# A hybrid mLSTM/GLA decoder block: the last MLP pass in seven products, the GLA state block-diagonal, and some work moved between engines

## The chip, the cores and the metric

The kernel runs on one core of a Trainium2 chip. The metric is the device time of one execution in microseconds (us). A core has five engines that run side by side and wait for each other by semaphores: TensorE (PE in the profile; its weight loads are listed as PEld) multiplies matrices into PSUM, VectorE (DVE) and ScalarE (ACT) work elementwise on PSUM and SBUF, GpSimd (POOL) works on SBUF alone and issues DMAs, SyncE (SP) issues DMAs. Three executions of the kernel before took 2819.16, 2821.59 and 2823.09 us.

## The reference

One decoder block over 2048 tokens of width 1024, all in float32:

1. Token mixing. RMSNorm of x, one combined projection, then two parallel head groups over chunks of tokens: an mLSTM (4 heads of 128, exponential input gate, running-max stabiliser) and a gated linear attention, GLA (4 heads, keys of 64, values of 128). In GLA each head has a state S of 64 x 128. Per chunk the output is o = A v + (q exp(b)) S, where A holds the causal products within the chunk and b the summed log decays, and then S = exp(b_last) S + k_w^T v. Both groups are normed per head and gated; their concatenation goes through w_out and is added to x.
2. Cross-attention on 256 memory rows, added to x.
3. MLP: x = x + square(relu(rmsnorm(x) w1)) w2, hidden width 4096.
4. A final RMSNorm with its own gain.

## The kernel before

The 2048 tokens are worked in four groups of 512 (GROUP); the first three run in a loop, the fourth is emitted with final=True. xres holds the residual rows of a group, four tiles i of 128 rows. Every weight comes as "slabs" of 128 x 512. SP loads them in pairs (512 KB) into raw; ACT copies a slab into w_hi (rounded; split_hi, L905), DVE subtracts that from raw into w_lo (split_lo, L1417 and L1419), and PE takes three matmuls for each product: hi x hi, hi x lo, lo x hi. Both rings have four slabs (RING), and the splits run three slabs ahead (LEAD). Each engine goes through the same numbered slabs, and all other work is written by hand between them: "if s == 49" in an engine's function means that this work is queued on that engine behind its split in slab step s. An engine's queue is strictly in order.

A full slab (slab, L1981) is 12 matmuls of 128 x 128 by 128 x 512: four output tiles by three. The projections of the mixing are slabs 0 to 55; w_out starts with slab 56.

GLA, in slab steps 41 to 53 (G_SLAB = 41, three steps a chunk, four chunks c of 128 tokens a group, so 16 chunks in all). PE's queue in step slot 0 holds, for the chunk before: outputs_start (carried for heads 0 and 2, L2135), state_step (L2166), outputs (carried for heads 1 and 3, L2135, and then the four A v products, L2157), and then levels for the next chunk (L2097, L2100), whose end signals lvl_full. The state stS has the key rows of two heads on the partitions 0 to 63 and 64 to 127, so each product of carried takes 64 rows of the array and 128 columns. DVE's queue in the same step: split_lo, then a wait on o_full and a copy of the output from PSUM into tok (L1744), a wait on s_full and two state updates (L1749), then two level_sum (L1564 multiply and L1568 reduce), which wait on lvl_full. ACT waits for that copy (o_out) and takes four sums of squares (L1226).

The gated mLSTM heads are moved in this way: in step 49, behind its split, DVE gates all four heads (gate_heads, 16 instructions, L1606), each head signalling mixed. POOL waits for all four and then issues 16 DMAs that move blocks of the heads between partitions (move_heads, L687). In step 53 DVE waits until all 16 have landed (heads_in) and transposes 32 x 32 blocks, ACT makes x_hi (L1099), DVE x_lo (L1585); heads 0 and 1 in step 53, heads 2 and 3 in step 54, with the split of step 54 between them. PE waits for the x_lo of all four before it starts slab 56.

The MLP goes over the hidden width in four passes hb of 1024 (LAST is 3). A pass has 16 full slabs for w1, and then h w2. In all passes but the last of the last group, h w2 is done in seven products of quarters (the Strassen-Winograd scheme; P1, P7, P6, P2, P5, P4, P3 in this order). A product is four slabs (product, L2348), each with 6 matmuls (two tiles by three). It needs sums of quarters of the weights (sums_dram, made once by POOL) and of the hidden rows: POOL makes these (hidden_sums) and the lower halves of the operands (operand_low, L727), ACT the upper halves (operand_high, L1306). DVE adds each finished quarter to xres (add_product, L1840) and signals prod_free. The pass is 16 + 28 slabs. The last pass of the last group (mlp_pass) is an ordinary one: 16 slabs for w1 and 16 full slabs for w2 (L1981, and last_chunks, L2329, which finishes one tile of rows after the other).

Behind it comes the final norm of the last group. For each tile i of rows DVE adds the last half (L1935), multiplies by the final gain (L1938), ACT takes the sum of squares of the half (L1092), DVE the variance (L1942), ACT a logarithm and an exponential (L1381, L1383), DVE three small refining steps (L1921 to L1924) and the scaling of one half (L1927), ACT the scaling of the other (L1373), and SP stores the row tile (L592). The first halves were squared and weighed while PE was still at work.

## Time and profile before

| what | value |
|---|---|
| median of 3 executions | 2821.59 us |
| the profiled execution, its device time | 2816.63 us |
| its span, first to last instruction | 2815.1 us |
| PE busy | 2796.2 us (99%) |
| PEld busy | 2328.2 us (83%) |
| DVE busy | 1812.2 us (64%) |
| ACT busy | 1514.2 us (54%) |
| POOL busy | 1054.5 us (37%) |
| mean granted TensorE clock | 0.999 |
| traffic of HBM | 346.24 MB read, 33.59 MB written |

The span is the time from the first to the last instruction of the profiled execution, and the device time lies 1.5 us above it. Busy means that an instruction of the engine is under way; matmuls overlap each other, so the distance between the starts of two matmuls, and not their length, is what one costs. An engine's idle time matters only where PE, or the end, waits for it.

### The profile page before, as it was taken

Reading aid. Unit: us, or ns where it says so; the run is one execution under the profiler, and the core shown is the slowest. Engines: PE = TensorE matmul, PEld = TensorE weight load, DVE = VectorE, ACT = ScalarE, POOL = GpSimd, SP = SyncE. Lnnn points to the kernel's source line nnn. Section 1 sums busy time; section 2 is a strip of 40 time slices with the busy share of each in tenths; the row PEclk is TensorE's granted clock in tenths of the full one; section 3 lists DMA queues with packets and bytes.
Section 4 is the critical chain, followed back from the end, with each engine's and each line's share of the span. In section 5 each row is a group of like instructions: output and inputs, shape, how many; then the busy total and the mean of one; then the engine's idle time right before and its main releaser. Section 6 shows DMA issues by size and latency. Waiting matters only on the chain.

```text
span 2815.1 us, 44964 instructions
## 1 busy us (share of the span) xinstructions
PE 2796.2 (99%) x15076; PEld 2328.2 (83%) x15076; DVE 1812.2 (64%) x3011; ACT 1514.2 (54%) x3126; POOL 1054.5 (37%) x1334
## 2 busy tenths in 40 slices
PE   8999999999999999999999999999999999999998
PEld 8888888888878888888888888888888888888887
DVE  6376764776686755556788675466668675545665
ACT  6555444566655444555565544456655544455553
POOL 5264554665354400234546320044435550013330
PEclk9999999999999999999999999999999999999999
DMA  6732476565552222355554222255455222234442
GB/s 216 251 105 67 173 268 242 186 211 151 149 188 83 76 89 90 108 171 161 164 177 135 69 84 90 90 158 179 143 150 199 81 74 90 90 104 144 151 149 83
DMA packets 185906, 393.41 MB, mean 140 GB/s; under 512 B 14224, under 2 KB 14368, under 8 KB 185664
## 3 DMA queue, kind: packets, MB, share of 16 engines
q1 hardware_dynamic: 160112, 309.89, 35.2%
q0 software_dynamic: 22880, 75.72, 8.0%
q10 hardware_dynamic: 2672, 4.76, 0.5%
q8 instruction: 129, 2.11, 0.3%
q14 instruction: 113, 0.93, 0.1%
HBM read 346.24 MB, written 33.59 MB: 135 GB/s over the span
## 4 chain that ended last, share of the span: by engine, by line
PE 98%; DMA 1%; ACT 0%; DVE 0%; issue 0%; POOL 0%; ACTq 0%; DVEq 0%
PE bank L1981 44%; PE work L1981 22%; PE bank L2348 17%; PE work L2348 3%; PE work L1995 1%; PE bank L2386 1%; PE work L2097 1%; DMA vo_dram<-folded 1%; PE bank L1995 1%; PE work L2135 1%; PE work L2157 1%; PE work L2043 1%; PE work L2246 1%; PE work L2250 1%; PE work L2245 1%; PE work L2229 1%
## 5 line engine op out<-in xcount | busy, mean ns | idle before, releaser
L905 ACT ACTIVATE w_hi<-raw 128x512 fp32r<-128x512 f32 x1156 | 724.7, 630 | 1012.6 <-PE bank L1981 514.5
L1419 DVE TENSOR_TENSOR w_lo<-raw,w_hi 128x512 fp32r<-128x512 f32 x657 | 481.2, 736 | 785.8 <-ACT w_hi L905 784.2
L1417 DVE SCALAR_TENSOR_TENSOR w_lo<-raw,w_hi 128x512 fp32r<-128x512 f32 x499 | 448.8, 921 | 92.6 <-ACT w_hi L905 91.6
L737 POOL TENSOR_TENSOR hr<-qk 128x256 f32<-128x256 f32 x60 | 44.9, 750 | 773.3 <-ACT qk L1293 773.3
L2348 PE MATMUL bank<-w_hi,h_hi 128*128 128x512 f32 x720 | 280.3, 389 | 0.1
L2348 PE MATMUL bank<-w_hi,h_lo 128*128 128x512 f32 x720 | 280.1, 389 | 0.0
L2348 PE MATMUL bank<-w_lo,h_hi 128*128 128x512 f32 x720 | 280.1, 389 | 0.0
L1981 PE MATMUL bank<-w_hi,x_hi 128*128 128x512 f32 x640 | 255.2, 399 | 0.0
L1981 PE MATMUL bank<-w_lo,x_hi 128*128 128x512 f32 x640 | 249.6, 390 | 0.0
L1981 PE MATMUL bank<-w_hi,x_lo 128*128 128x512 f32 x640 | 249.5, 390 | 0.0
L727 POOL TENSOR_TENSOR h_lo<-qk,h_hi 128x256 fp32r<-128x256 f32 x180 | 180.7, 1023 | 71.1 <-ACT h_hi L1306 71.1
L1981 PE MATMUL work<-act_hi,w_hi 128*128 128x512 f32 x512 | 199.2, 389 | 0.0
L1981 PE MATMUL work<-act_lo,w_hi 128*128 128x512 f32 x512 | 199.2, 389 | 0.0
L1981 PE MATMUL work<-act_hi,w_lo 128*128 128x512 f32 x512 | 199.2, 389 | 0.0
L1981 PE MATMUL bank<-act_hi,w_hi 128*128 128x512 f32 x464 | 180.8, 390 | 0.0
L1981 PE MATMUL bank<-act_hi,w_lo 128*128 128x512 f32 x464 | 180.5, 389 | 0.0
L1981 PE MATMUL bank<-act_lo,w_hi 128*128 128x512 f32 x464 | 180.5, 389 | 0.0
L2348 PEld LDWEIGHTS bank<-w_hi,h_hi 128*128 128x128 f32 x720 | 135.1, 188 | 28.8 <-issue 0.7
L2348 PEld LDWEIGHTS bank<-w_hi,h_lo 128*128 128x128 f32 x720 | 135.1, 188 | 28.2
L2348 PEld LDWEIGHTS bank<-w_lo,h_hi 128*128 128x128 f32 x720 | 135.1, 188 | 27.9
L791 POOL TENSOR_TENSOR zz<-zz,gqkv 128x128 f32<-128x128 f32 x224 | 118.0, 564 | 106.8 <-ACT gqkv L1251 106.8
L1981 PE MATMUL bank<-x_hi,w_hi 128*128 128x512 f32 x384 | 152.9, 398 | 0.0
(405 smaller groups left out, 6465.0 us busy)
## 6 DMA issues: line engine op xcount, KB each, us to landing
raw<-in_w_dram SPq DMA_DIRECT2D x226, 512.0 KB, 3.9
raw<-sums_dram SPq DMA_DIRECT2D x120, 512.0 KB, 3.9
raw<-in_w_in_dram SPq DMA_DIRECT2D x112, 512.0 KB, 3.5
raw<-in_w_out_dram SPq DMA_DIRECT2D x32, 512.0 KB, 4.1
raw<-kq_dram SPq DMA_DIRECT2D x32, 512.0 KB, 3.8
raw<-vo_dram SPq DMA_DIRECT2D x32, 512.0 KB, 3.8
xres<-in_x_dram POOLq DMA_DIRECT2D x16, 512.0 KB, 5.9
early_rows<-in_w_dram POOLq DMA_DIRECT2D x8, 1024.0 KB, 8.8
```

The lines of the kernel that those rows point to most:

```text
L727: nc.gpsimd.tensor_tensor(operand(q, h_lo)[:, kt, :], src, operand(q, h_hi)[:, kt, :].bitcast(F32), ALU.subtract).then_inc(operand_lo_pool, 1)
L737: nc.gpsimd.tensor_tensor(diff[:, kt, :], quarter(0, 0, kt), quarter(0, 1, kt), ALU.subtract).then_inc(diff_ready, 1)
L791: ins = nc.gpsimd.tensor_tensor(v[:, :, :, r, :], v[:, :, :, r, :], src, ALU.mult)
L905: nc.scalar.activation(w_hi[:, slot, :], raw[:, pair_slot, slot % 2, :], ACT.Copy).then_inc(slab_hi, 1)
L1417: ins = stt(out=w_lo[:, slot, :], in0=src, scalar=1.0, in1=hi, op0=ALU.mult, op1=ALU.subtract)
L1419: ins = tt(w_lo[:, slot, :], src, hi, ALU.subtract)
L1981: ins = mm(dst, left, right, start=(kt == 0 and j == 0), stop=(kt == KT - 1 and j == 2))
L1995: ins = transpose(into[kt % 4][:, i * P:(i + 1) * P], src[:, i, kt * P:(kt + 1) * P], ident[:])
L2043: ins = mm(wbank[2 + j % 2][:, hh * MEM:(hh + 1) * MEM], left, right, start=(k == 0 and i == 0), stop=(k == 1 and i == 2))
L2097: ins = mm(dst, z, z, start=True, stop=True)
L2135: ins = mm(work[:, 2, cut[hd]], qe[p0:p0 + 64, c % 2, j, :], stS[p0:p0 + 64, j, :], start=(hd == 0), stop=False, skip_group_check=True)
L2348: ins = mm(dst[:], left[:, kt, here], right[:, kt, :], start=(CHAIN_BEFORE[q] is None and kt == 0 and j == 0), stop=(kt == HALF - 1 and j ...
```

## The change

1. The last pass of the last group is a pass of seven products like the others; mlp_pass, last_chunks and their semaphores and tables go. In its last product P3 the order over tiles and slabs is written out, so that tile 0 is complete six matmuls before tile 1. P4 gives the left half of row tiles 2 and 3 and P3 the right half of row tiles 0 and 1; so the rows are finished in the order 2, 3, 0, 1 (LAST_ROWS).
2. POOL multiplies the four halves that are complete early (P2 and P5) by the final gain, behind the hidden sums of the pass. ACT takes their sums of squares in the slab steps 34 and 38. DVE does the halves of P4 in one instruction each (row by scale by gain) and those of P3 as before in two. The final rows lie in x_blocks and no longer in qk.
3. The GLA state stS becomes 128 x 256 for each pair of heads, with zeros off the diagonal. carried is two matmuls of all 128 rows and 256 columns in outputs_start, and nothing of it in outputs. The state update on DVE is four instructions of 64 partitions in place of two of 128.
4. The copy of the GLA output into tok is ACT's, in front of its sums of squares; DVE no longer waits on o_full there.
5. gate_heads for the heads 2 and 3 of the mLSTM is queued in step 50, behind the level sums of that step.

The rest of the diff puts nine small tiles into one, keeps the addresses behind them where they were (SPARE) and drops what is not used any more.

```diff
-FINAL_USES, _ = use_table([KT] * 4)
+LAST_ROWS = (2, 3, 0, 1)
 assert len(USES) == GROUP_SLABS and GROUP_SLABS % (2 * PAIRS) == 0
...
         stC = sb("stC", [P, HEADS, HD + 1])
-        stS = sb("stS", [P, 2, HD])
+        stS = sb("stS", [P, 2, 2 * HD])
...
         x_blocks = sb("x_blocks", [P, NCH, D], F32, mlp)
+        last_rows = x_blocks
         x_turned = sb("x_turned", [P, KT, GROUP], F32, mlp)
...
-                    if hb < LAST or not final:
-                        for name, row, col in WEIGHTS:
-                            if name == "sums":
-                                for k in range(HALF):
-                                    sums_done(sp, HALF * hb + k)
-                            w = sums_dram if name == "sums" else A["w2"]
-                            for kp in range(HALF // 2):
-                                load(g, p, pair_of(w, hb * D + row * COLS + kp * 2 * P, col * COLS))
-                                p += 1
-                    else:
-                        for b in range(2):
-                            for kp in range(KT // 2):
-                                load(g, p, pair_of(A["w2"], hb * D + kp * 2 * P, b * COLS))
-                                p += 1
+                    for name, row, col in WEIGHTS:
+                        if name == "sums":
+                            for k in range(HALF):
+                                sums_done(sp, HALF * hb + k)
+                        w = sums_dram if name == "sums" else A["w2"]
+                        for kp in range(HALF // 2):
+                            load(g, p, pair_of(w, hb * D + row * COLS + kp * 2 * P, col * COLS))
+                            p += 1
...
                 if final:
-                    for i in range(NCH):
-                        sp.wait_ge(tok_ready, PRO_ROWS + 8 * g + i + 1)
-                        sp.wait_ge(half_out, i + 1)
-                        sp.dma_start(out[g * GROUP + i * P:g * GROUP + (i + 1) * P, :], out_rows[:, i, :])\
+                    for k, i in enumerate(LAST_ROWS):
+                        sp.wait_ge(tok_ready, PRO_ROWS + 8 * g + k + 1)
+                        sp.wait_ge(half_out, k + 1)
+                        sp.dma_start(out[g * GROUP + i * P:g * GROUP + (i + 1) * P, :], last_rows[:, i, :])\
                             .then_inc(stored_last, 16)
...
                     hidden_sums(2)
+                    hidden_sums(3)
+                    pool.wait_ge(fin_g_in, 16 * NG)
+                    for q in (Q_P2, Q_P5):
+                        for tile in range(2):
+                            i, here = 2 * ROW_HALF[q] + tile, slice(COL_HALF[q] * COLS, (COL_HALF[q] + 1) * COLS)
+                            pool.wait_ge(prod_free, free_no(g, LAST, q, tile))
+                            nc.gpsimd.tensor_tensor(last_rows[:, i, here], xres[:, i, here], fin_g[:, here],
+                                                    ALU.mult).then_inc(first_half, 1)
                     return
...
-                def sum_half(i, half):
+                def sum_half(i, half, into):
 
                     here = slice(half * COLS, (half + 1) * COLS)
                     nc.scalar.activation(tok[:, i, here], xres[:, i, here], ACT.Square,
-                                         accum_out=(ss, ss_b)[half][:, i:i + 1]).then_inc(half_ss, 1)
+                                         accum_out=into[:, i:i + 1]).then_inc(half_ss, 1)
...
                     if slot == 0 and 1 <= c <= NCH:
 
-                        act.wait_ge(o_out, 4 * g + c)
+                        act.wait_ge(o_full, 4 * g + c)
+                        nc.scalar.activation(tok[:, c - 1, COLS:], work[:, 2, :], ACT.Copy).then_inc(o_out, 1)
...
-                        split(g, MLP_AT[hb] + s)
+                        if not (final and hb == LAST and s + LEAD >= PASS_SLABS):
+                            split(g, MLP_AT[hb] + s)
...
+                        if final and hb == LAST and s in (2 * KT + 18, 2 * KT + 22):
+                            q = Q_P2 if s == 2 * KT + 18 else Q_P5
+                            for tile in range(2):
+                                act.wait_ge(prod_free, free_no(g, LAST, q, tile))
+                                sum_half(2 * ROW_HALF[q] + tile, COL_HALF[q], ss)
                         if final:
...
                     if slot == 0 and 1 <= c <= NCH:
-                        dve.wait_ge(o_full, 4 * g + c)
-                        nc.vector.tensor_copy(tok[:, c - 1, COLS:], work[:, 2, :]).then_inc(o_out, 1)
                         dve.wait_ge(s_full, 4 * g + c)
                         if c >= 2:
                             dve.wait_ge(s_ready, 4 * g + c - 1)
-                        for j in range(2):
-                            ins = stt(out=stS[:, j, :], in0=stS[:, j, :], scalar=eb[:, (c - 1) % 2, j, CH - 1:CH],
-                                      in1=work[:, 3, j * HD:(j + 1) * HD], op0=ALU.mult, op1=ALU.add)
+                        for hd in range(HEADS):
+                            j, k, half = hd // 2, hd % 2, slice(64 * (hd % 2), 64 * (hd % 2) + 64)
+                            own = stS[half, j, k * HD:(k + 1) * HD]
+                            ins = stt(out=own, in0=own, scalar=eb[half, (c - 1) % 2, j, CH - 1:CH],
+                                      in1=work[half, 3, j * HD:(j + 1) * HD], op0=ALU.mult, op1=ALU.add)
                         ins.then_inc(s_ready, 1)
...
                     if s == 49:
                         read_out(dve, g, 4 * B_MO + 3)
                         dve.wait_ge(num_out, 4 * g + 4)
-                        gate_heads(0, HEADS)
+                        gate_heads(0, HEADS, (0, 1))
+                    if s == 50:
+                        gate_heads(0, HEADS, (2, 3))
...
+                    if final and hb == LAST:
+                        return
...
+                def weigh_half(q, tile):
+
+                    i, half = 2 * ROW_HALF[q] + tile, COL_HALF[q]
+                    here = slice(half * COLS, (half + 1) * COLS)
+                    dve.wait_ge(prod_free, free_no(g, LAST, q, tile))
+                    return tt(last_rows[:, i, here], xres[:, i, here], fin_g[:, here], ALU.mult)
+
+                for hb in range(HB):
                     split_pass(hb)
-                if final:
-                    mlp_pass()
-                def last_row(i):
-
+
+                def last_var_of(k):
+
+                    here = slice(LAST_ROWS[k], LAST_ROWS[k] + 1)
+                    dve.wait_ge(half_ss, NCH + k + 1)
+                    stt(out=var[:, here], in0=ss_b[:, here], scalar=1.0 / D, in1=ss[:, here], op0=ALU.mult,
+                        op1=ALU.add).then_inc(last_var, 1)
+
...
+                def last_row(k):
+
+                    i = LAST_ROWS[k]
                     here = slice(i, i + 1)
-                    dve.wait_ge(last_guess, i + 1)
+                    half = slice(COLS, D) if i < 2 else slice(0, COLS)
+                    dve.wait_ge(last_guess, k + 1)
...
+                    dve.wait_ge(last_scale, k + 1)
+                    if k < 2:
+                        dve.wait_ge(prod_free, free_no(g, LAST, Q_P4, k))
+                        stt(out=last_rows[:, i, half], in0=xres[:, i, half], scalar=rstd[:, here], in1=fin_g[:, half],
+                            op0=ALU.mult, op1=ALU.mult).then_inc(tok_ready, 1)
+                    else:
+                        ts(last_rows[:, i, half], last_rows[:, i, half], rstd[:, here], None, ALU.mult)\
+                            .then_inc(tok_ready, 1)
...
+                    dve.wait_ge(fin_g_in, 16 * NG)
+                    dve.wait_ge(half_ss, NCH)
+                    link(ts(ss[:], ss[:], 1.0 / D, EPS, ALU.mult, ALU.add))
+                    last_var_of(0)
+                    last_var_of(1)
+                    for k in range(2):
+                        last_row(k)
+                    add_product(LAST, Q_P3, 0)
+                    add_product(LAST, Q_P3, 1)
+                    link(weigh_half(Q_P3, 0))
+                    last_var_of(2)
+                    link(weigh_half(Q_P3, 1))
+                    last_row(2)
+                    last_var_of(3)
+                    last_row(3)
                     return
...
-                def carried(c, hds):
-
-                    for hd in hds:
-                        j, p0 = hd // 2, 64 * (hd % 2)
-                        ins = mm(work[:, 2, cut[hd]], qe[p0:p0 + 64, c % 2, j, :], stS[p0:p0 + 64, j, :],
-                                 start=(hd == 0), stop=False, skip_group_check=True)
-                    return ins
+                def carried(c, j):
+
+                    return mm(work[:, 2, j * 2 * HD:(j + 1) * 2 * HD], qe[:, c % 2, j, :], stS[:, j, :],
+                              start=(j == 0), stop=False, skip_group_check=True)
...
                     stand_alone(pe)
-                    carried(c, (0, 2)).then_inc(o_even, 1)
+                    for j in range(2):
+                        carried(c, j)
 
                 def outputs(c):
 
                     pe.wait_ge(at_full, 4 * g + c + 1)
-                    pe.wait_ge(o_even, 4 * g + c + 1)
                     stand_alone(pe)
-                    carried(c, (1, 3))
...
+                    if final and hb == LAST and q == Q_P3:
+                        for tile, kt in ((0, 0), (1, 0), (0, 1), (1, 1), (0, 2), (0, 3), (1, 2), (1, 3)):
+                            if kt == 0:
+                                pe.wait_ge(prod_free, free_no(g, hb, Q_P5, tile))
+                            if tile == 0:
+                                pe.wait_ge(slab_lo, slab_no(g, MLP_AT[hb] + 2 * KT + HALF * q + kt + 1))
+                                pe.wait_ge(operand_lo_pool, per_pass(g, N_POOL_LOW, hb, HALF * POOL_LOW[q] + kt + 1))
+                            here = slice(tile * P, (tile + 1) * P)
+                            for j, (left, right) in enumerate(((hi, w_hi), (hi, w_lo), (lo, w_hi))):
+                                ins = mm(chain_bank(q, tile)[:], left[:, kt, here], right[:, kt, :], start=False,
+                                         stop=(kt == HALF - 1 and j == 2), skip_group_check=True)
+                            if kt == HALF - 1:
+                                ins.then_inc(prod_full, 1)
+                        return
```

## Rows read from the trace of the kernel before

**Rows 1.** The page, section 4: the chain that ended last, by engine
```profile
PE 98%; DMA 1%; ACT 0%; DVE 0%; issue 0%; POOL 0%; ACTq 0%; DVEq 0%
```

**Rows 2.** Timeline of PE, a chunk's output: start us, length us, engine, line, instruction, count
```profile
265.07 0.39 PE L1981 MATMUL bank<-w_hi,x_lo 128*128 128x512 f32 x1
265.39 0.71 PE L2135 MATMUL work<-stS,qe 64*128 64x128 f32 x4
266.03 0.66 PE L2166 MATMUL work<-gqkv,kwT 128*64 128x128 f32 x8
266.62 0.71 PE L2135 MATMUL work<-stS,qe 64*128 64x128 f32 x4
267.26 1.16 PE L2157 MATMUL work<-gqkv,sg 128*128 128x128 f32 x8
```

**Rows 3.** Timeline of PE, a slab followed by mLSTM matmuls of the whole array
```profile
193.74 0.39 PE L1981 MATMUL bank<-x_hi,w_lo 128*128 128x512 f32 x1
193.97 1.05 PE L2229 MATMUL work<-qk 128*128 128x128 f32 x8
194.86 0.60 PE L2233 MATMUL work<-ident,qk 128*128 128x128 f32 x4
```

**Rows 4.** Timeline of DVE, slab steps 49 and 50 of the first group
```profile
293.57 4.28 DVE L1606 SCALAR_TENSOR_TENSOR qk<-tok,hscale,qk 128x128 f32<-128x128 f32 x16
...
298.97 0.59 DVE L1749 SCALAR_TENSOR_TENSOR stS<-stS,eb,work 128x128 f32<-128x128 f32 x2
299.49 0.61 DVE L1564 TENSOR_TENSOR mw<-work,lvl_mask 128x448 f32<-128x448 f32 x1
...
301.00 0.62 DVE L1564 TENSOR_TENSOR mw<-work,lvl_mask 128x448 f32<-128x448 f32 x1
```

**Rows 5.** Timeline of PE, the end of the levels in slab step 50
```profile
298.12 0.30 PE L2100 MATMUL work<-gqkv 64*64 64x64 f32 x8
```

**Rows 6.** Timeline of POOL, the moves of the heads; in brackets idle before and releaser
```profile
298.55 10.37 POOL L687 DMA_DIRECT2D qk<-qk  x16 [5.45 <-DVE qk L1606]
```

**Rows 7.** Line L687 by itself, first group: from issue to landing
```profile
DMA to landing us min/median/max: 2.2/2.8/4.4
```

**Rows 8.** Timeline of DVE, slab steps 53 and 54
```profile
313.35 1.30 DVE L1581 STREAM_TRANSPOSE tok<-qk 128x512 f32<-128x512 f32 x2
...
318.35 1.42 DVE L1585 SCALAR_TENSOR_TENSOR x_lo<-tok,norm_g,x_hi 128x512 fp32r<-128x512 f32 x2 [0.20 <-ACT x_hi L1099]
```

**Rows 9.** Timeline of PE, the first matmul of slab 56
```profile
320.22 0.39 PE L1981 MATMUL work<-w_hi,x_hi 128*128 128x512 f32 x1
```

**Rows 10.** Windows behind PE's end: stretch, length, busy by engine, PEclk, DMA share, GB/s
```profile
2807.50:2809.90 2.40, 0.13 (x1) 0.00 (x0) 1.98 (x8) 1.90 (x7) 0.00 (x0) 1.00 0.40 164
2810.10:2815.00 4.90, 0.00 (x0) 0.00 (x0) 1.31 (x5) 1.40 (x2) 0.00 (x0) 0.50 0.68 280
```

**Rows 11.** Timeline of PE, the first matmuls of the kernel
```profile
6.99 3.65 PE L2014 MATMUL work<-ident 128*128 128x128 f32 x16 [6.99 <-ACT tok L948]
```

**Rows 12.** Timeline of PE, the last pass: its first and its last matmul
```profile
2720.43 0.39 PE L2386 MATMUL bank<-act_hi,w_hi 128*128 128x512 f32 x1
...
2807.24 0.39 PE L2329 MATMUL work<-w_hi,h_lo 128*128 128x512 f32 x1
```

**Rows 13.** Timeline of DVE and ACT, last row tile: last refining step, last scaling
```profile
2810.84 0.16 DVE L1924 SCALAR_TENSOR_TENSOR rstd<-y 128x1 f32<-128x1 f32 x1
...
2811.03 0.72 ACT L1373 ACTIVATE qk<-qk,rstd 128x512 f32<-128x512 f32 x1 [0.26 <-DVE rstd L1924]
```

**Rows 14.** Timeline of DVE, the products of the pass before
```profile
2708.67 3.56 DVE L1417 SCALAR_TENSOR_TENSOR w_lo<-raw,w_hi 128x512 fp32r<-128x512 f32 x3
...
2716.47 0.74 DVE L1840 SCALAR_TENSOR_TENSOR xres<-bank,rs_mlp,xres 128x512 f32<-128x512 f32 x1
```

**Rows 15.** Timeline of POOL, its last work in the pass before
```profile
2710.49 4.18 POOL L727 TENSOR_TENSOR h_lo<-hr,h_hi 128x256 fp32r<-128x256 f32 x4
```

**Rows 16.** Lines of POOL by form: busy us, mean ns, then idle before
```profile
L718 POOL TENSOR_TENSOR tok<-tok 128x512 f32<-128x512 f32 x6 | 8.1, 1345 | 0.5
```

153 lines of the change are left out of this document (20 added, 133 removed).

## The prediction

> **What bounds the kernel now.** I read four views in this order. The chain of waits first: 98% of the span is TensorE's own work [rows 1]. So PE's stream of matmuls is the time, plus the tail behind its last matmul; work on the other engines counts only where PE or the tail waits for it. Then PE's timeline around every place that the change touches, then the timelines of DVE, ACT and POOL there, to see how late each handover to PE is, and last the windows behind PE's end. The profiled execution took 2816.63 us (span 2815.1), and the sum is made against it; the median of the runs shown, 2821.59, lies 4.96 above, and I add that at the end.
>
> **The seven products, on PE.** The old last pass has 32 full slabs of 12 matmuls, 384; from its first to its last matmul there are 383 distances in 2807.24 - 2720.43 = 86.81 us, 0.2267 each [rows 12]. The new one has 16 x 12 + 7 x 24 = 360. 24 x 0.2267 = -5.44 us. The chain [rows 1] shows no stall inside the passes of that kind, so I take no stall in the stream itself; the tail is below.
>
> **GLA on PE.** From the last slab matmul before a chunk's output to the A v products it is 267.26 - 265.07 = 2.19 us: 0.96 to L2166, 0.59 for L2166, 0.64 for the second L2135 [rows 2]. The four matmuls of each L2135 (two passes for each of two heads) take 0.64. Eight float32 matmuls of the whole array take 194.86 - 193.97 = 0.89, so 0.111 each, and start 0.23 after the slab [rows 3]. Four at 0.111 would be 0.44: going into and out of the 64-row form costs 0.2 a time. The new carried has four passes of twice the columns, 4 x 0.222 = 0.89, starts 0.23 behind the slab and pays once, 0.09, before L2166: 0.23 + 0.89 + 0.09 + 0.59 = 1.80. Gain 0.39 a chunk, 1.56 a group, 6.2 in all. Bounds: 0 if the passes of 256 columns were slowed as the small forms are, 0.45 if the wider pass saves its fixed part as well. I take 0.39, the rows being of the same form. But this gain only counts if PE does not wait before slab 56, and that is the next part.
>
> **The gating a slab later.** This is the step that decides. PE starts slab 56 at 320.22 [rows 9], and needs the x_lo of all four moved heads. DVE ends the last of them at 318.35 + 1.42 = 319.77 [rows 8]: 0.45 us to spare. The chain before it: gating ends at 293.57 + 4.28 = 297.85 [rows 4]; POOL starts issuing 0.70 later and needs 10.37 for 16 DMAs, one after the other [rows 6]; so the last issue starts at 308.27, and landing takes 2.2 to 4.4 [rows 7], up to 312.7; DVE goes on with the transposes at 313.35 [rows 8], about 0.7 us later.
>
> In the new kernel, in the clock of the old trace:
> - Two chunks are behind PE at step 50, so it is 0.78 early, and the first half of the gating starts near 292.8. A gating instruction is 4.28/16 = 0.27, half are 2.14: 294.9.
> - The split of step 50 takes 0.56 (split and copy share the 1.12 from 297.85 to 298.97 [rows 4]): 295.5. The copy is gone.
> - Four state updates, 0.26 each like the old two (0.52 together): 296.6. Bounds 0.13 (half the partitions, half the time) and 0.30 each.
> - The level sums wait for PE's levels, which end at 298.12 + 0.30 [rows 5], now three chunks of 0.39 earlier: 297.25. Two sums at 301.00 - 299.49 = 1.51 [rows 4]: 300.3.
> - Only now the second half of the gating: 302.4, against 297.85.
> - POOL: + 0.70 + 9.72 to the last issue, 312.8. Landing 2.8 (2.2 to 4.4): 315.6 (315.0 to 317.2).
> - The transposes start 2.3 late; the rest of the chain keeps its 6.42 (313.35 to 319.77), since ACT and DVE have nothing else in it: 322.0. PE starts slab 56 at 322.1.
>
> PE arrives there at 320.22 - 4 x 0.39 = 318.7, so it stands for 3.4 us. Against the old start that is +1.9 a group (0.7 if the level sums do not wait and the landing takes 2.2; 3.5 if it takes 4.4). With four groups: **+7.6 us** (3 to 14), and the 6.2 of GLA are in it already: they are lost in the wait. Behind slab 56 everything is moved by the same amount. ACT now copies the output itself, 0.7 us a chunk, in front of squares for which it had waited for DVE: nothing. The wait of DVE for its level masks in step 51 would also be shorter; that is lost in the same stall.
>
> The clock: behind PE's end the granted clock is still 1.00 for 2.4 us and then 0.50, which is 1.2 GHz in place of 2.4 [rows 10]. A stand of 3.4 us is longer than that. At the start of the kernel 16 transposes took 3.65 us [rows 11], 0.23 each and so twice the 0.111 of rows 3; that stretch at the lower level lost some 1.8 us. I take a fall in three stands of four: 3 x 1.8 = **+5.4** (0 to 7.4). The Trainium skill (TensorE: Matmul & The Clock Gate, section Why this matters for your kernels) says that an idle gap in the middle of a kernel drops the clock to half; by it all four stands would pay, by the old trace taken alone, which has no such gap inside, none need to.
>
> **The last pass's side work and the tail.** Before: from PE's end (2807.24 + 0.23 = 2807.47) the last scaling starts 3.56 later, ends at 4.28, and the execution's span closes at 7.6, so the last store costs 3.3 [rows 12, 13]. In the new kernel, E is the end of PE's stream, and in the pass before E is 2720.43:
> - POOL ends its operands at 2710.49 + 4.18 = E - 5.8 [rows 15] and then weighs four halves. 1.35 each for 128x512 [rows 16], up to 1.8 beside DVE: until about E + 1.
> - While POOL works DVE's splits take 3.56/3 = 1.19 in place of 0.6 [rows 14]; ACT's four extra sums (0.7 each) hold its splits of slabs 38 and 42 by 1.1 to 1.4. Slab 43's lower half comes at about E - 1.7, against a need at E - 2.0; a stall of 0.4 at most, which I leave in the tail.
> - The add of P4 tile 0 starts at 2716.47 = E - 4.0 in the old order [rows 14]; now about E - 1.7, and tile 1 ends at E - 0.35.
> - Then DVE alone, in its written order: variances of rows 2 and 3 (each behind a sum of 0.8 and behind the other's logarithm and exponential on ACT, 0.2 each) until E + 1.3; last_row twice (three small steps of 0.2, one product of 0.7): E + 4.0; two adds of 0.7: E + 5.4; weigh, variance, weigh: E + 7.0; last_row: E + 8.1. Row 3's variance needs ACT's sum, which waits behind the scaling of row 1 in ACT's queue: E + 8.2; logarithm, exponential, three small steps: the last scaling starts at E + 9.4.
> That is 5.9 later than the 3.56 of before. If POOL slows nobody and P4's adds stay at E - 4.0, the same count gives 3.5; if it costs more at each step, 7. I take **+5.3**, near the upper side, because both the queue order and the shared time of POOL and DVE are in rows.
>
> The Trainium skill (GPSIMD Engine Reference, section 1. Specifications) says that POOL shares its SBUF interfaces with DVE when DVE has two SBUF inputs; the 1.19 against 0.6 of the split agrees. By it the weighing on POOL is paid by DVE.
>
> **Sum.** +7.6 + 5.4 - 5.4 + 5.3 = +12.9: 2829.5 for the profiled execution, 2834.5 for the median.
>
> **Rivals.**
> - *The clock holds.* Same stands, no fall. For: no clock below 1.00 inside the old trace. Against: rows 10. Sum +7.5: 2829.1.
> - *The heads still come in time* (the other side). Then PE keeps the 6.2 of GLA and a further 0.2 a group in step 51. This needs the second gating to be over by 298 to 299, so level sums that do not sit in front of it, or DMAs that land 2 us sooner. Against it: DVE's queue is in order, and even with no wait for levels the work in front adds 4.7 us to a chain with 1.2 to spare. Sum -7.0 - 5.4 + 5.3 = -7.1: 2814.5. It decides from a landing before 313.4.
> - *The last pass starves.* POOL's weighing and ACT's sums hold the splits so long that PE waits for slabs 38 to 43 as well, 1 to 1.5 us each for three of them. Against: a slab of a product lasts 6 x 0.2267 = 1.36, and the splits run three slabs, 4.1 us, ahead, so a delay of 1.1 to 1.4 is mostly covered. Sum +12.9 + 4: 2838.5.
> - *The block-diagonal state brings nothing*, because 256 columns cost more than 0.222. It would not show: up to 0.39 a chunk vanishes in the stand before slab 56. It is no case of its own.
>
> **How the numbers follow.** Chances: forecast 0.50, the clock holds 0.25, the heads in time 0.17, starving 0.08. A run of this kernel can tell 0.2%, 5.6 us, from no change. Slower by more: 0.46 of the forecast, 0.17 of the clock case (its lower part, with stands of 2 us, is below 5.6), 0.07 of the starving one: 0.70. Same: 0.04, 0.07, 0.03 and 0.01: 0.15. Faster: 0.14 of the case in time and 0.01: 0.15. The range starts at 2817, which leaves out the better half of the heads case, and ends at 2842 (stands of 4.5 us with four falls and a tail of 7 would be 2846).
>
> **What would show it.** Line L687's 16 issues start some 4.5 us later against PE's slabs, and DVE's transposes wait for a DMA. PE's waits have a new row at the first matmul of slab 56, released by DVE x_lo, four times, 3 to 4 us each; windows there show PEclk below 1.00. L2135 goes, two matmuls with 256 columns stand in its place, 0.9 us in all, and L2166 starts 1.2 after the slab. The last pass has 360 matmuls, and the last scaling starts 9 us after PE's end. The prediction is wrong if PE enters slab 56 without a wait, if a wait is under 2 us, or if the tail is no longer than before.

## The result, and the profile after

The changed kernel takes 2836.19 us (median of 6 runs, 2830.17 to 2839.95), the kernel before 2821.16 (6 runs): ratio 1.0053, 95% interval 1.004 to 1.0066. It is 15.0 us slower; forecast were 12.9. The profiled execution (2839.95 us, span 2838.4) is the longest of the six, 23.3 us above the profiled one of before. That is 8.3 us more than the medians differ by: it lies 3.8 above its own median, and the profiled execution of before lies 4.5 under its own. One of the seven executions of e12 below took 16079.09 us and is left out of that kernel's ratio.

PE's waits of the kernel after (line that waited <- what released it: us in all, times, longest):

```profile
PE work L1949 <- DVE x_lo L1562: 14.0, 4, 3.9
PE work L2145 <- issue: 3.8, 2, 3.0
PE work L1949 <- DVE x_lo L1413: 0.7, 1, 0.7
PE bank L2295 <- DVE w_lo L1394: 0.7, 1, 0.7
```

The first row is new. Four times, once a group, PE stands at the first matmul of slab 56. The path to it, on DVE and POOL, kernel after (start, duration, engine, line, operation; in brackets the idle time before and what ended it):

```profile
292.24 2.18 DVE L1583 SCALAR_TENSOR_TENSOR qk<-tok,hscale,qk 128x128 f32<-128x128 f32 x8
294.34 0.68 DVE L1396 TENSOR_TENSOR w_lo<-raw,w_hi 128x512 fp32r<-128x512 f32 x1
294.94 1.42 DVE L1726 SCALAR_TENSOR_TENSOR stS<-stS,eb,work 64x128 f32<-64x128 f32 x4
296.94 0.62 DVE L1541 TENSOR_TENSOR mw<-work,lvl_mask 128x448 f32<-128x448 f32 x1 [0.57 <-PE work L2068]
...
299.97 2.18 DVE L1583 SCALAR_TENSOR_TENSOR qk<-tok,hscale,qk 128x128 f32<-128x128 f32 x8
...
314.82 1.30 DVE L1558 STREAM_TRANSPOSE tok<-qk 128x512 f32<-128x512 f32 x2 [4.46 <-DMA qk<-qk]
...
319.83 1.41 DVE L1562 SCALAR_TENSOR_TENSOR x_lo<-tok,norm_g,x_hi 128x512 fp32r<-128x512 f32 x2 [0.20 <-ACT x_hi L1091]
```

```profile
302.85 10.34 POOL L671 DMA_DIRECT2D qk<-qk  x16 [11.09 <-DVE qk L1583]
```

Against [rows 4]: the gating that was one block of 16 ending at 297.85 is now two of 8, and between them stand a split, four state updates, a wait for PE's levels and the level sums. The second ends at 302.15; POOL starts its 16 issues at 302.85 instead of 298.55 [rows 6], and the transposes wait 4.46 us for a DMA. At PE:

```profile
317.77 0.39 PE L1949 MATMUL bank<-w_hi,x_lo 128*128 128x512 f32 x1
321.47 0.49 PE L1949 MATMUL work<-w_hi,x_hi 128*128 128x512 f32 x1 [3.31 <-DVE x_lo L1562]
```

The distance is 3.70 us where matmuls follow each other at 0.23; in the other groups 3.59, 3.95 and 4.30. The granted clock there (columns: stretch, its length, busy and instructions of PE, PEld, DVE, ACT, POOL, then PEclk, DMA share and GB/s):

```profile
318.00:320.00 2.00, 0.16 (x1) 0.00 (x0) 1.80 (x5) 1.35 (x4) 0.00 (x0) 1.00 0.16 25
320.00:322.00 2.00, 0.53 (x2) 0.48 (x3) 1.25 (x2) 1.97 (x3) 0.00 (x0) 1.00 0.68 238
322.00:324.00 2.00, 2.00 (x6) 1.58 (x5) 1.58 (x3) 1.43 (x4) 0.00 (x0) 0.50 0.00 0
324.00:326.00 2.00, 2.00 (x7) 1.55 (x7) 1.84 (x5) 1.98 (x3) 0.00 (x0) 0.64 0.00 0
326.00:330.00 4.00, 4.00 (x19) 3.30 (x18) 3.22 (x12) 2.18 (x4) 2.85 (x4) 1.00 0.61 209
```

The clock is still full while PE stands, and is down at 1.2 GHz from 322.0, just after the restart. From 0.64 in 324 to 326 it follows that the low stretch ends near 325.4: 3.4 us at half speed, 1.7 lost. In group 2 it is down during the stand already, and for longer:

```profile
1672.00:1676.00 4.00, 2.92 (x13) 2.06 (x11) 3.80 (x8) 2.29 (x5) 0.00 (x0) 1.00 0.00 0
1676.00:1680.00 4.00, 1.53 (x4) 1.26 (x5) 2.66 (x5) 3.89 (x6) 0.00 (x0) 0.64 0.38 131
1680.00:1684.00 4.00, 4.00 (x11) 3.17 (x10) 3.09 (x8) 3.40 (x6) 0.00 (x0) 0.51 0.00 0
```

That is 6.8 us, of which 5.5 come after the restart at 1678.5: 2.7 lost.

GLA (see [rows 2] for before), and then the last pass and tail:

```profile
264.86 0.39 PE L1949 MATMUL bank<-w_hi,x_lo 128*128 128x512 f32 x1
265.09 1.02 PE L2101 MATMUL work<-stS,qe 128*128 128x256 f32 x4
266.05 0.66 PE L2130 MATMUL work<-gqkv,kwT 128*64 128x128 f32 x8
266.63 1.16 PE L2121 MATMUL work<-gqkv,sg 128*128 128x128 f32 x8
```

```profile
2818.32 5.20 DVE L1394 SCALAR_TENSOR_TENSOR w_lo<-raw,w_hi 128x512 fp32r<-128x512 f32 x3
2823.45 1.40 DVE L1819 SCALAR_TENSOR_TENSOR xres<-bank,row_cols,xres 128x512 f32<-128x512 f32 x2
...
2828.90 1.40 DVE L1819 SCALAR_TENSOR_TENSOR xres<-bank,row_cols,xres 128x512 f32<-128x512 f32 x2
```

```profile
2818.29 6.38 POOL L857 TENSOR_TENSOR x_blocks<-xres,fin_g 128x512 f32<-128x512 f32 x4
```

```profile
2823.58 0.51 PE L2295 MATMUL bank<-w_hi,h_hi 128*128 128x512 f32 x1 [0.72 <-DVE w_lo L1394]
```

```profile
2833.36 1.43 ACT L1349 ACTIVATE x_blocks<-x_blocks,row_cols 128x512 f32<-128x512 f32 x2
```

From the last slab matmul to the A v products it is 266.63 - 264.86 = 1.77 us, 2.19 before. The last pass takes 83.28 us instead of 87.04, the tail behind PE's end (2825.77) 12.65 instead of 7.60.

**Where the 23.3 us are.** By PE's own marks in the two profiles, each number the extra over before: group 0 +5.3, group 1 +6.6, group 2 +6.6, group 3 up to the last pass +3.8; last pass -3.8; tail +5.1. They add to 23.6; 0.1 is gained at the start, the rest is rounding. How much of the groups' 22.2 us belongs to slab 56 can be read directly: from the first matmul of slab 42 to the first of slab 56, a distance that holds GLA's outputs, and over the 30 matmuls behind that, where the clock is low. Each number is the extra over the same distance in before:

| us | group 0 | group 1 | group 2 | group 3 | all |
|---|---|---|---|---|---|
| slab 56 starts later, GLA's gain already in | 1.48 | 1.38 | 1.71 | 2.13 | 6.7 |
| the clock behind it | 1.74 | 1.47 | 2.70 | 1.60 | 7.5 |

That is 14.2 us, where 7.6 + 5.4 = 13.0 were forecast. Another 5.0 have nothing to do with slab 56: the second group ends in a gap of 3.40 us that no wait explains (row "issue" above; the two such gaps of before were 1.0 and 1.4, the other one of after 1.15), followed by 6.8 us at the low clock, of which 2.9 are lost. In group 0 PE waits once more at 341 us, for another x_lo (0.7 in the rows above), which costs 1.0. The last 1.9 come in steps of under 0.6 us, for which I have no cause. The gaps of before at the groups' edges, then the stretches behind the long one of after:

```profile
PE work L2181 <- issue: 1.6, 2, 1.0
```

```profile
1472.00:1476.00 4.00, 2.67 (x6) 1.90 (x7) 1.75 (x6) 2.71 (x7) 0.00 (x0) 0.54 0.53 156
1476.00:1480.00 4.00, 4.00 (x12) 2.77 (x11) 4.00 (x4) 0.00 (x0) 1.15 (x2) 0.61 0.34 130
```

### The profile page after: what moved, and what is told of

The parts are those of the page before. It is cut to its first block, busy times and chain, and to the rows that moved or that the text cites. A ratio compares the mean times of both kernels' runs of the same rounds, so it can differ in the third digit from the quotient of the medians.

```text
span 2838.4 us, 44957 instructions
## 1 busy us (share of the span) xinstructions
PE 2796.6 (99%) x14988; PEld 2325.1 (82%) x14988; DVE 1836.9 (65%) x3035; ACT 1537.5 (54%) x3182; POOL 1081.2 (38%) x1370
## 4 chain that ended last, share of the span: by engine, by line
PE 92%; DVE 3%; issue 1%; POOL 1%; ACT 1%; DMA 1%; DVEq 0%; ACTq 0%; POOLq 0%
PE bank L1949 41%; PE work L1949 22%; PE bank L2312 17%; PE work L2312 3%; POOL qk L671 1%; PE work L1963 1%; PE bank L2350 1%; DVE w_lo L1394 1%; PE work L2065 1%; PE work L2011 1%; PE bank L1963 1%; PE work L2210 1%; PE work L2214 1%; PE work L2209 1%; PE work L2193 1%
## 5 line engine op out<-in xcount | busy, mean ns | idle before, releaser
L897 ACT ACTIVATE w_hi<-raw 128x512 fp32r<-128x512 f32 x1168 | 732.9, 630 | 1014.1 <-PE bank L1949 511.8
L1394 DVE SCALAR_TENSOR_TENSOR w_lo<-raw,w_hi 128x512 fp32r<-128x512 f32 x525 | 480.5, 938 | 98.4 <-ACT w_hi L897 97.7
L2312 PE MATMUL bank<-w_hi,h_hi 128*128 128x512 f32 x760 | 296.4, 390 | 0.5
L2312 PE MATMUL bank<-w_hi,h_lo 128*128 128x512 f32 x760 | 295.8, 389 | 0.0
L2312 PE MATMUL bank<-w_lo,h_hi 128*128 128x512 f32 x760 | 295.7, 389 | 0.0
L711 POOL TENSOR_TENSOR h_lo<-qk,h_hi 128x256 fp32r<-128x256 f32 x192 | 189.1, 1005 | 80.2 <-ACT h_hi L1299 80.2
L2312 PEld LDWEIGHTS bank<-w_hi,h_hi 128*128 128x128 f32 x760 | 142.6, 188 | 33.0 <-issue 3.6
L2312 PEld LDWEIGHTS bank<-w_hi,h_lo 128*128 128x128 f32 x760 | 142.6, 188 | 29.5
L2312 PEld LDWEIGHTS bank<-w_lo,h_hi 128*128 128x128 f32 x760 | 142.7, 188 | 29.5
```

Of the source, the lines that this page charges most:

```text
L711: nc.gpsimd.tensor_tensor(operand(q, h_lo)[:, kt, :], src, operand(q, h_hi)[:, kt, :].bitcast(F32), ALU.subtract).then_inc(operand_lo_pool, 1)
L897: nc.scalar.activation(w_hi[:, slot, :], raw[:, pair_slot, slot % 2, :], ACT.Copy).then_inc(slab_hi, 1)
L1394: ins = stt(out=w_lo[:, slot, :], in0=src, scalar=1.0, in1=hi, op0=ALU.mult, op1=ALU.subtract)
L2312: ins = mm(dst[:], left[:, kt, here], right[:, kt, :], start=(CHAIN_BEFORE[q] is None and kt == 0 and j == 0), stop=(kt == HALF - 1 and j ...
```

## The experiments

Each ratio is against executions of the kernel before that ran beside it, in three series: e1 to e4, e5 to e8 and e9 to e12. The kernel before had medians of 2818.75, 2816.55 and 2818.73 us in them, so between series ratios are compared and not times. Profiles are compared by PE's marks: start of a group, of the last pass, PE's end.

**e1: all four gatings in step 49 again**, the rest as after.

```diff
-                        gate_heads(0, HEADS, (0, 1))
-                    if s == 50:
-                        gate_heads(0, HEADS, (2, 3))
+                        gate_heads(0, HEADS, (0, 1, 2, 3))
```

> The changed kernel with all four gatings in step 49 again; nothing else differs. Theory (the late gating makes the heads land late, PE stands before slab 56 and its clock falls): no wait of PE on x_lo before slab 56, no clock fall there, and GLA's 0.39 us a chunk kept; against the changed kernel -(3.7 to 4.3 of standing - 0.2) - 1.7 to 3.4 of clock, per group, so -21 to -26 us; against the kernel before -6 (GLA) - 3.8 (last pass) + 5 (tail) = -5, ratio 0.998. Rival (the stand has another cause, such as the wider GLA state or ACT's copy): the stand stays, ratio near 1.005.

2812.30 us, ratio 0.9979 (0.997 to 0.9988). Where the last eight gatings stand in DVE's queue turns a kernel that is 0.5% slower into one that is 0.2% faster. PE's waits:

```profile
PE work L2063 <- DVE mw L1541: 1.7, 3, 0.6
PE work L2063 <- issue: 0.5, 1, 0.5
```

No wait for x_lo is left and the clock stays at 1.00 up to PE's end. What is left is 0.5 us a group in step 51, where PE, now earlier, waits for the level masks. From the start to the last pass e1 is 4.6 us shorter than before in the profiles: 16 chunks of 0.42 are 6.7 us, less this wait of 2.2. Last pass 82.24, tail 13.58.

**e2: only the gatings moved**, in the kernel before.

```diff
-                        gate_heads(0, HEADS)
+                        gate_heads(0, HEADS, (0, 1))
+                    if s == 50:
+                        gate_heads(0, HEADS, (2, 3))
```

> The kernel before with only the gating of heads 2 and 3 in step 50. Theory: the second half ends some 4.7 to 5 us later (split, copy, state update, two level sums in front of it), against 0.7 us to spare at the landing and 0.45 at slab 56: stand of 3.3 to 4 us a group plus 1.7 or more of clock, +20 us, ratio 1.006 to 1.008. Rival (the stand needs the faster GLA of the changed kernel): no stand, ratio 1.000.

2836.64 us, ratio 1.0066 (1.0052 to 1.008), as expected. That edit alone costs the whole loss and more, since here no gain of GLA is set against it.

```profile
PE work L1983 <- DVE x_lo L1585: 11.8, 4, 3.3
```

The clock falls in three of the four groups. In group 0 it does not, after a distance of 3.19 us; in groups 1, 2 and 3 it does, after 3.19, 3.27 and 3.68 us. So the same stand can go either way.

**e3: only the last pass and its tail new**; old GLA, gatings in 49.

```diff
-        stS = sb("stS", [P, 2, 2 * HD])
+        stS = sb("stS", [P, 2, HD])
...
+                        nc.vector.tensor_copy(tok[:, c - 1, COLS:], work[:, 2, :]).then_inc(o_out, 1)
```

(and the old carried and state update)

> The kernel before with only the new last pass and tail (old GLA state, copy by DVE, gatings in step 49). Theory: the last pass is 3.8 us shorter (24 matmuls less 1.7 of waiting for w_lo), the tail 5.0 longer: +1.3 us, ratio 1.0005, the same. Rival (the tail costs little, the gain of the pass is lost in the mixing of the changed kernel): -3 to -5 us, ratio 0.9985. The difference to the run with all gatings in step 49 is GLA: 6 us by the theory.

2819.86 us, ratio 1.0004 (0.9995 to 1.0013): no change. The pass takes 83.38 us (-3.7), the tail 12.64 (+5.0). From e3 to e1, 7.6 us by the medians, is GLA's part when nothing takes it away; 6.2 were forecast. e3's profile has one gap of 2.4 us at a group's edge with a fall of the clock behind it, which may be the difference; that is not shown.

**e4: PE kept busy in the stand**: the kernel after, with 16 transposes of the identity, whose result nothing reads, before the wait for x_lo.

```diff
                     if s == B_OUT * KT:
+                        for _ in range(16):
+                            transpose(wbank[3][:, 0:P], ident[:], ident[:])
                         pe.wait_ge(act_lo_ready, TRS * g + PRO_TR + 4)
```

> The changed kernel with 16 transposes of the identity into an unused bank queued on PE before its wait for the x_lo of slab 56 (3.5 us of PE at full clock, work that the result does not need). Theory (the stand is paid twice, once as time and once as a lower clock behind it): slab 56 starts at the same time as in the changed kernel or up to 0.5 later, no fall of the clock there, 1.7 to 3.4 us less a group: -7 to -12 us, ratio to before near 1.002. Rival (the clock's fall costs nothing, as PE is not the bound in the microseconds behind it): ratio unchanged at 1.005 or higher.

2827.37 us, ratio 1.0031 (1.0019 to 1.0042). By the ratios this is 6.2 us less than after (8.8 by the times, but the kernel before was 2.4 us faster in this series), though slab 56 cannot start sooner. The intervals of the two ratios just overlap (after's begins at 1.004). The 16 transposes took only 1.75 us of PE and not the 3.5 expected, so a good part of the stand stayed idle, 7.5 us in all where it was 14.0:

```profile
PE work L1949 <- DVE x_lo L1562: 7.5, 4, 2.3
```

The granted clock is low in two stretches of 3.4 us, both after a restart; in after it was low in five, three of 3.4 and two of 6.8 us (one of these at the group's edge). Behind the four stands after loses 7.5 us by the clock and e4 3.7. So 3.8 of the 7.5 us between the two profiles (spans 2838.4 and 2830.9) are the clock behind the stands. 5.0 more are after's gap at the edge with its fall, which this edit did not touch and which e4's profile does not have; against them slab 56 starts 0.5 later in all, and e4 has a wait of 1.3 of its own in an MLP pass. The seven executions of e4 have mean granted clocks of 0.997 to 0.999, the six of after 0.994 to 0.996, so the profile is no exception. The clock was a cost of its own, and about two fifths of the loss (1.0053 to 1.0031) can be had back without moving the heads at all. Two stands of e4 still brought a fall, each behind only 1.8 us of idle time, while one of 2.3 us did not.

**e5: the second half of the gating in step 50, but ahead of the state update and the level sums.**

```diff
+                    if s == 50:
+                        gate_heads(0, HEADS, (2, 3))
                     c, slot = divmod(s - G_SLAB, 3)
                     if slot == 0 and 1 <= c <= NCH:
                         dve.wait_ge(s_full, 4 * g + c)
```

> The changed kernel with the second half of the gatings still in slab step 50, but queued ahead of the state update and the two level sums (behind the split of the step before). Theory (it is the work in front in DVE's queue, not the step, that makes the heads late): gatings end near the time of before, the moves land in time, no stand before slab 56: 23 us less than the changed kernel, ratio to before 0.998, as with all gatings in step 49. The wait of PE on the level masks in step 51 (0.5 us a group with all gatings in step 49) should stay much the same, since the level sums are behind 16 gatings again. Rival (a step later is too late in any order): stand of 2 us or more, ratio above 1.002.

2815.07 us, ratio 0.9994 (0.9985 to 1.0003). Expected was 0.998. The stand is gone, as in e1. DVE:

```profile
294.59 0.68 DVE L1396 TENSOR_TENSOR w_lo<-raw,w_hi 128x512 fp32r<-128x512 f32 x1
295.19 2.19 DVE L1583 SCALAR_TENSOR_TENSOR qk<-tok,hscale,qk 128x128 f32<-128x128 f32 x8
297.29 1.43 DVE L1728 SCALAR_TENSOR_TENSOR stS<-stS,eb,work 64x128 f32<-64x128 f32 x4
298.75 0.62 DVE L1541 TENSOR_TENSOR mw<-work,lvl_mask 128x448 f32<-128x448 f32 x1
```

The second gating ends at 297.38 here and at 302.15 in after. It was not the step that cost, but the place in DVE's queue inside the step. Its profile (span 2811.7) does not differ from e1's (2811.6); the ratio is 0.15% worse, with intervals that touch only at their ends. Part of that is the series: one and the same kernel, e7 and e12, came out at 0.998 in this series and at 0.9971 in the third. And the same edit made to e7 costs nothing (e8, in this series). So e5 shows that the stand is gone; that it is faster than the kernel before its own ratio does not show.

**e6: side work of the last pass spread** (on e1): ACT's four early sums one a step in steps 38 to 41 instead of two by two in 34 and 38, POOL's weighing only after the last w_lo.

```diff
+                    pool.wait_ge(slab_lo, slab_no(g, GROUP_SLABS))
-                    for q in (Q_P2, Q_P5):
+                    for q in (Q_P5, Q_P2):
...
-                        if final and hb == LAST and s in (2 * KT + 18, 2 * KT + 22):
-                            q = Q_P2 if s == 2 * KT + 18 else Q_P5
-                            for tile in range(2):
+                        if final and hb == LAST and 2 * KT + 22 <= s < 2 * KT + 26:
+                            q, tile = (Q_P2 if s < 2 * KT + 24 else Q_P5), s % 2
```

> All gatings in step 49, and in the last pass ACT takes its four early sums of squares one a step in steps 38 to 41, and POOL weighs its halves only when the last w_lo of the kernel is made, P5 before P2. Theory (POOL beside DVE's splits and ACT's pairs of sums delay the last w_lo and P4's adds): PE's last pass at 360 x 0.2267 = 81.6 us without a wait (0.6 to 1.7 less), P4's adds start near E - 4 instead of E - 2.3, and the tail behind PE falls from 12.6 to 13.6 us to about 10: 3 to 5 us less than with the gatings alone, ratio to before 0.9965. Rival (the tail is long by DVE's written order alone): PE's wait goes, the tail stays above 12, ratio 0.9975.

2813.57 us, ratio 0.999 (0.9981 to 0.9999): short of what I expected. The stream did what was expected: 81.60 us from the first matmul of the pass to PE's end, 5.44 less than before and without a wait. But the tail stayed, 13.15 us where e1 had 13.58. P4's adds come 1.65 sooner (2793.08 = PE's end - 3.97), and POOL's products, which now lie later, hold two small instructions of DVE for 1.0 and 1.1 us, where in e1 it was one, 1.0: -1.65 + 1.1 is about the -0.43 measured. ACT's and POOL's work were moved at once, so which of the two freed the stream is not shown.

**e7: also the order of the tail** (on e6): each add of P3 goes between the variances and rows, and every row ends in one product by rstd and fin_g.

```diff
                     last_var_of(0)
+                    add_product(LAST, Q_P3, 0)
                     last_var_of(1)
-                    for k in range(2):
-                        last_row(k)
-                    add_product(LAST, Q_P3, 0)
-                    add_product(LAST, Q_P3, 1)
-                    link(weigh_half(Q_P3, 0))
+                    last_row(0)
+                    add_product(LAST, Q_P3, 1)
                     last_var_of(2)
-                    link(weigh_half(Q_P3, 1))
+                    last_row(1)
```

> The run before with DVE's last instructions in another order (P3 tile 0 is added as soon as it is there, tile 1 before the row 1 of the order) and every last half done in one instruction (row by scale by gain) in place of two. Theory (order costs too): the last scaling starts about E + 5.5, the tail about 9 us, 1 to 2 us less than the run before: ratio to before 0.996. Rival (ACT's chain of sum, logarithm and exponential is what ends last): no change against the run before.

2811.82 us, ratio 0.998 (0.9971 to 0.9989), where 0.996 and a tail of about 9 us were expected. Tail 11.23 us. DVE and POOL in it:

```profile
2795.11 1.17 DVE L1874 SCALAR_TENSOR_TENSOR row_cols<-row_cols 128x1 f32<-128x1 f32 x1
...
2797.47 1.27 DVE L1883 SCALAR_TENSOR_TENSOR row_cols<-row_cols 128x1 f32<-128x1 f32 x1
```

```profile
2793.71 5.02 POOL L858 TENSOR_TENSOR x_blocks<-xres,fin_g 128x512 f32<-128x512 f32 x4 [0.72 <-issue]
```

Two instructions of 128x1, which take 0.16 elsewhere, take 1.2 while POOL multiplies. The tail's gain of 1.9 over e6 comes from this edit, the new order and the single product together.

**e8: e7 with the gatings of e5.**

> The run before with the second half of the gatings in step 50 in front of the state update, as in the first run of this series: the candidate that keeps every gain. Theory: 0 to 2 us less than with all in step 49, ratio to before 0.995 to 0.996.

2811.71 us, ratio 0.9981 (0.9972 to 0.999), the same as e7 and not the 0.995 to 0.996 expected. In one group of its profile PE waits 0.6 us for x_lo, so the margin at slab 56 is thin.

**e9 and e10: DVE weighs the early halves instead of POOL**, on e1 and on e7, in steps 34, 35, 38 and 39; **e11 and e12** are e1 and e7 once more.

```diff
-                    for q in (Q_P2, Q_P5):
-                        for tile in range(2):
-                            ...
-                            nc.gpsimd.tensor_tensor(last_rows[:, i, here], xres[:, i, here], fin_g[:, here],
-                                                    ALU.mult).then_inc(first_half, 1)
+                        if final and hb == LAST and s in (34, 35, 38, 39):
+                            if s == 34:
+                                dve.wait_ge(fin_g_in, 16 * NG)
+                            weigh_half(Q_P2 if s < 38 else Q_P5, s % 2).then_inc(first_half, 1)
```

> The kernel of e1 (all four gatings in step 49) with one edit: VectorE weighs the four early halves by fin_g, 0.68 us each, in steps 34, 35, 38 and 39 of the last pass, and GpSimd none. Theory (what the last pass lost of its 5.44 us and part of its longer tail are GpSimd's four products: beside them three w_lo took 4.66 us instead of 2.0, and the 128x4 instruction behind them 1.18 instead of 0.2): P4's adds start 4 us before the last matmul instead of 2.3, P3's adds 3.3 us sooner, the wait of 0.3 to 0.7 us on a bank in P3 goes; together about 3.8 us less than e1, a tail of about 10.3 us where e1 had 13.6. Rival (VectorE was the full engine there, and the four products only move onto it): w_lo come later in the stream, TensorE waits 1 to 2 us more in the last pass, and the time is that of e1 or 1 us above it.

> The kernel of e7 (order of the tail changed) with the same edit as e9. Theory: in e7 two small VectorE instructions of the tail took 1.17 and 1.27 us instead of 0.16 beside GpSimd's products, and the order now follows the last matmul: 2 us less than e7, a tail of 9.2 us instead of 11.2. Rival: as for e9, no gain or 1 us of loss.

> The kernel of e1 once more, as the measure for e9 in one call, since the kernel before itself came out 2.2 us apart in the two calls so far. Expected: 6.0 us (ratio 0.9979) under the kernel before; if e1's gain was partly a drift of the call, 4 us.

> The kernel of e7 once more beside e1's. Its profile had a tail 2.4 us shorter than e1's (11.2 against 13.6), and the stream before was the same to 0.6 us, so 2.4 us under e1 is expected; the rival is that the 1.0 to 1.8 us gap at the edge of a group and other unwaited gaps vary from run to run by as much, and the medians are the same to 1 us.

e9 2814.03 us, ratio 0.9983 (0.9974 to 0.9992); e11, its measure, 2813.67, 0.9982 (0.9973 to 0.9991). e10 2811.39, 0.9975 (0.9965 to 0.9984); e12, its measure, 2810.91, 0.9971 (0.9959 to 0.9983). Taking the work from POOL gains nothing by the medians, as the rival says. In e9:

```profile
2785.96 1.22 DVE L1862 TENSOR_TENSOR x_blocks<-xres,fin_g 128x512 f32<-128x512 f32 x1
2787.11 1.22 DVE L1387 SCALAR_TENSOR_TENSOR w_lo<-raw,w_hi 128x512 fp32r<-128x512 f32 x1
...
2793.65 0.68 DVE L1862 TENSOR_TENSOR x_blocks<-xres,fin_g 128x512 f32<-128x512 f32 x1
2794.44 0.69 DVE L1387 SCALAR_TENSOR_TENSOR w_lo<-raw,w_hi 128x512 fp32r<-128x512 f32 x1
2795.05 0.68 DVE L1862 TENSOR_TENSOR x_blocks<-xres,fin_g 128x512 f32<-128x512 f32 x1
2795.66 0.69 DVE L1387 SCALAR_TENSOR_TENSOR w_lo<-raw,w_hi 128x512 fp32r<-128x512 f32 x1
```

While POOL still makes its operands (up to 2792) the first two halves cost DVE 1.22 each; behind that 0.68. DVE has next to no idle time left in this stretch, and P4's adds start at 2796.26 = PE's end - 2.3 as in e1. The tail is 12.6 in e9 and 10.8 in e10 against 13.6 and 11.2. In e10 the longer pass takes that back and more: 82.85 us, where e12's is 81.60. In e9 it does not: the pass is 82.48 against e11's 82.24, so pass and tail together are 0.7 shorter in the profiles, and the medians show nothing of it. Expected tails were 10.3 and 9.2: I had counted the products where they went away and not where they came.

e12 lies 2.8 us under e11 by the medians (expected 2.4). Between these two lie both edits, the side work spread and the tail's order: in the profiles the pass is 0.6 shorter and the tail 2.4, and 1.9 of the tail's 2.4 is the step from e6 to e7. It is the fastest version here, 7.8 us under the kernel before.

## Why the prediction was right

**The place of the time** was right: the loss comes from the stand in front of slab 56 and the clock behind it, by an edit that alone costs it (e1, e2). The chain by its steps, group 0, forecast and then measured: first half starts 292.8, 292.24; ends 294.9, 294.34; state updates 0.26 each, 0.36; level sums begin 297.25, 296.94, behind a wait of 0.57 for PE's levels, as foreseen; second half ends 302.4, 302.15; transposes 315.6, 314.82; slab 56 322.1, 321.47. Only the state update was outside its bounds (0.13 to 0.30): a 64x128 instruction lasts 0.35 us and a 128x128 one 0.34, and their starts lie 0.36 apart where those of before lay 0.26. It cost nothing else, since the level wait behind it absorbed it.

**The stand** was 3.4 forecast; the four distances are 3.59 to 4.30, each 0.23 of it a normal step, so the idle part is 3.4 to 4.1. PE also arrived 0.7 earlier than forecast (318.0, not 318.7), and that lengthens the stand without costing anything. What counts is how much later slab 56 starts: 6.7 us in all against the +7.6 of this step, inside its bounds and a little under its value.

**The clock** was the term that was too small. Forecast were three falls of 1.8 us, 5.4. After's profile has four in the stands, and one of them lasts twice as long: 7.5. A further 2.9 went at the group's edge. e2 had three falls of 3.4 us. So the number of falls was a fair mean and their length was not always 3.4. The Trainium skill (TensorE: Matmul & The Clock Gate, section Why this matters for your kernels) says that an idle gap drops the clock in the middle of a kernel; these runs agree in seven stands out of eight (after 4 of 4, e2 3 of 4), and in e4 work which nobody reads wins back 6.2 us by the ratios. How long a stand is does not settle it alone: of the two of 3.19 us in e2 one brought a fall and one did not.

**GLA's matmuls**: 0.39 a chunk forecast, 2.19 - 1.77 = 0.42 measured. The four passes of 256 columns and the way out of them are 266.05 - 265.09 = 0.96. With the 0.09 for the way out that the prediction assumed it is 0.22 each, as forecast: the shape cost nothing extra. That this gain is lost in the stand is shown by e1: when the stand goes, it comes out.

**The last pass**: -5.44 less at most 0.4 forecast, -3.76 measured. This stall was the second mis-sized term. The three splits beside POOL's products took 5.20/3 = 1.73 each, where I had taken 1.19 from rows with 256 columns on POOL; of the 1.68 us lost 0.9 is the gap before slab 43's matmuls and the rest small gaps around it. e6 has the full 5.44. The size hangs on when POOL comes to its products: in after it starts them at PE's end - 7.5, ends 1.1 before PE and lies beside three splits; in e1, with the same last pass, it starts at PE's end - 6.2 and runs 0.2 past it. There the pass is 1.0 shorter (82.24) and the tail 0.9 longer (13.58), which is nearly the same sum.

**The tail**: +5.3 forecast, +5.05 measured. The last scaling was to start at PE's end + 9.4 and started at + 8.3 (2834.07), while the last store took longer. P4's adds came at PE's end - 2.3, forecast - 1.7, - 4.0 before, so 1.7 later, and up to 1.7 us of the 5.05 is theirs. POOL's part behind PE's end, which I had put in, was not there in after (the 128x4 instruction took 0.15) and was 1.0 in e1; e9 has it away again, 13.6 to 12.6. DVE's written order, with the two instructions for a half, is the largest part that a run shows, 1.9 us between e6's tail and e7's. The rest, some 1.4 us, was not tested.

**Rivals.** "The heads in time" is what e1 and e5 are, and both give it its mechanism: no stand and a full clock. e1's time is below the kernel before, e5's is not clear of it. Its condition was named as level sums not in front of the gating, and e5 meets just that. It was priced at -7.1; e1 is -5.9 by its ratio. "The clock holds" happened in one stand of eight. "The last pass starves" did not happen as priced, 4 us: the waits there cost 1.7, and the pass was shorter than before.

**How near, and how much of it luck.** The four terms were 7.6, 5.4, -5.4 and 5.3 and came out at 6.7, 7.5, -3.8 and 5.1. That adds to 15.5, and the medians differ by 15.0. The place and the signs were right by their mechanism. That the sum was only 2.1 off is luck in part: errors of +2.1 and +1.6 stand against -0.9 and -0.2, and for the gap at the group's edge, 5.0 us in after's profile, there was no term at all.

**Open.** The gap at a group's edge, 0.6 to 3.4 us over all profiles with no releaser shown, and why it sometimes ends in a fall of the clock. No kernel was made to test it. It moves single profiles by up to 5 us, which is why verdicts go by ratios of medians.

## What to carry to other kernels

Before moving work "a step later", write down what already stands in that step ahead of it in the engine's queue, waits on other engines above all: here the step was harmless, and the state updates and level sums in front of the moved instructions cost 0.6 to 0.7% of the kernel (after against e5 and e1). Price a stand of TensorE in the middle twice, once as idle time and once as the slower clock behind it, and if it can't be removed, filling it wins part of that back. Moving small work between DVE and POOL when both are working on large tiles moves its cost with it; look first at the order of the tail.

## What was not expected of the hardware

- The granted clock fell at very different points of like stands: in after 2.3 us after PE's last matmul in one, 2.8 in another, 3.9 and 4.0 in the others, there 0.2 us before the restart and 0.5 after it; it then stayed low for 3.4 us, in one stand for 6.8. After a distance of 3.19 us it fell in one group of e2 and held in another, and in e4 and e3 it fell behind idle times of only 1.8 and 2.0 us.
- DVE's 128x512 split with two inputs: one lasts 0.68 us alone, 1.22 to 1.27 beside POOL's 256-column operands, 1.77 to 1.82 beside POOL's 512-column product. Even 128x1 instructions went from 0.16 to 1.17 and 1.27 us.
- Half the partitions save no time: a 64x128 state update lasts 0.35 us, one of 128x128 0.34, and four of the small ones follow each other at 0.36 where the large ones did at 0.26.
- A float32 pass of 256 columns with the whole array ran at the same rate per column as one of 128, and the two groups of 64-row matmuls that it replaced, with the changes into and out of that form, cost 0.42 us a chunk more. How that divides between the form and its changes is not shown.
